# A mixer block and a hybrid layer on one core: row loads placed later in SP's program, and the last squares of a norm added on VectorE

## What is computed

```
# first block
m = sigmoid(ga) * (ya @ w_a_out) + sigmoid(gb) * (yb @ w_b_out)      # "wa", "wb"
x = x + m @ w_o                                                      # "wo"
gate = sigmoid(rmsnorm(x, ple_norm_g) @ w_ple_gate)                  # "gate"
x = x + gate * (p @ w_ple_proj)                                      # "proj"
# second block
mod = silu(c) @ w_ada + b_ada          # 2048 -> 3 * 2048, one row of c
shift, scale, gate = split(mod, 3)
h = rms_norm(x, g) * (1 + scale) + shift
... attention and retention from h @ w_in, then @ w_out
```

## Time and profile before

| what | value |
|---|---|
| time, median of 3 | 2500.03 us (2499.55 to 2504.28) |
| time of the profiled execution | 2501.74 us |
| its span, first to last instruction | 2500.2 us |
| granted TensorE clock, mean | 0.998 |
| PE busy | 2482.1 us (99%) |
| DVE busy | 1586.4 us (63%) |
| ACT busy | 975.8 us (39%) |
| POOL busy | 150.5 us (6%) |
| loads of modulation rows | 192 |

### The profile page before, as it was taken

How to read it: one execution, slowest core, us unless ns; L and a number is a source line. 1 busy time by engine, 2 the same in 40 slices (tenths; PEclk the granted TensorE clock), 3 DMA queues, 4 the chain that set the end, 5 groups by cost and what they waited for, 6 DMA issues and landing times.

```text
span 2500.2 us, 34300 instructions
## 1 busy us (share of the span) xinstructions
PE 2482.1 (99%) x13766; PEld 2112.9 (85%) x13766; DVE 1586.4 (63%) x2608; ACT 975.8 (39%) x1331; POOL 150.5 (6%) x195
## 2 busy tenths in 40 slices
PE   9999999999999999999989999999999999999999
PEld 8888888888889999988868788888888888888888
DVE  7656744567698888777677763585356555665435
ACT  6633325333344434432222353443344444444423
POOL 0011110012100000000001203200000000000001
PEclk9999999999999999999999999999999999999999
DMA  5333333333434434498688633336222344333532
GB/s 192 110 97 96 92 108 94 96 92 102 129 93 161 134 129 138 139 338 273 244 278 295 231 93 101 93 93 187 85 76 76 95 116 108 107 107 115 177 101 101
DMA packets 226686, 343.30 MB, mean 137 GB/s; under 512 B 68128, under 2 KB 87456, under 8 KB 223072
## 3 DMA queue, kind: packets, MB, share of 16 engines
q1 hardware_dynamic: 220480, 329.33, 42.0%
q10 hardware_dynamic: 1728, 8.81, 0.9%
q0 software_dynamic: 4320, 2.99, 0.5%
HBM read 308.01 MB, written 20.97 MB: 132 GB/s over the span
## 4 chain that ended last, share of the span: by engine, by line
PE 98%; DVE 1%; DMA 1%; issue 0%; ACT 0%; POOL 0%; SPq 0%; DVEq 0%; ACTq 0%; POOLq 0%
PE bank L397 79%; PE bank L558 4%; PE bank L557 4%; PE bank L556 4%; PE bank L1715 1%; PE bank L1714 1%; PE bank L1713 1%; PE bank L1039 0%; DMA RAW<-in_w_o 0%; PE bank L1098 0%; PE bank L1023 0%; DMA SG<-gates_dram 0%; POOL AC L2860 0%; PE bank L1101 0%; PE bank L1066 0%
## 5 line engine op out<-in xcount | busy, mean ns | idle before, releaser
L397 PE MATMUL bank<-XH,WL 128*128 128x512 f32 x2392 | 926.3, 389 | 8.5 <-DVE WL L470 8.5
L397 PE MATMUL bank<-XH,WH 128*128 128x512 f32 x2392 | 930.1, 391 | 0.0
L397 PE MATMUL bank<-XL,WH 128*128 128x512 f32 x2392 | 925.4, 389 | 0.0
L470 DVE TENSOR_TENSOR WL<-RAW,WH 128x1024 fp32r<-128x1024 f32 x366 | 454.5, 1243 | 487.2 <-ACT WH L432 486.6
L432 ACT CAST WH<-RAW 128x1024 fp32r<-128x1024 f32 x366 | 383.3, 1048 | 856.0 <-PE bank L397 765.3
L397 PEld LDWEIGHTS bank<-XH,WL 128*128 128x128 f32 x2392 | 449.5, 188 | 103.0 <-DVE WL L470 9.8
L397 PEld LDWEIGHTS bank<-XH,WH 128*128 128x128 f32 x2392 | 449.8, 188 | 92.6 <-issue 0.2
L397 PEld LDWEIGHTS bank<-XL,WH 128*128 128x128 f32 x2392 | 449.6, 188 | 92.3 <-issue 0.5
L397 PE MATMUL bank<-WH,XL 128*128 128x512 f32 x384 | 149.4, 389 | 0.0
L397 PE MATMUL bank<-WH,XH 128*128 128x512 f32 x384 | 149.4, 389 | 0.0
L397 PE MATMUL bank<-WL,XH 128*128 128x512 f32 x384 | 149.4, 389 | 0.0
(11 more groups left out here) (389 smaller groups left out, 3015.7 us busy)
## 6 DMA issues: line engine op xcount, KB each, us to landing
RAW<-in_w_in SPq DMA_DIRECT2D x239, 512.0 KB, 3.8
RAW<-in_w_in SPq DMA_DIRECT2D x130, 256.0 KB, 3.0
ASX<-in_w_ada SPq DMA_DIRECT2D x108, 256.0 KB, 5.5
AST<-in_w_ada SPq DMA_DIRECT2D x84, 256.0 KB, 5.4
RAW<-in_w_o SPq DMA_DIRECT2D x32, 512.0 KB, 5.9
RAW<-in_w_gate SPq DMA_DIRECT2D x32, 512.0 KB, 3.8
RAW<-in_w_out SPq DMA_DIRECT2D x32, 512.0 KB, 3.8
gates_dram<-OUT ACTq DMA_DIRECT2D x8, 1024.0 KB, 4.5
```

Of the source, the lines that this page charges most:

```text
L397: ins = nc.tensor.matmul(bank[b][:, cols], l, r[:, cols], start=first, stop=final)
L470: nc.vector.tensor_tensor(low_of(m), RAW[:, m % NRAW], high_of(m).bitcast(F32), ALU.subtract).then_inc(lo.sem, lo.step(m))
```

## The change

It has three parts.

1. `ada_sp` gets nine empty pieces after its first seven rows, so that each later row load stands that much later in SP's program. With it the first of the four loads of SG moves from the list of reloads (`reload_rest`) to the beginning of wb 0, as the other three stand.
2. POOL adds squares 1 to 12 only. Squares 13, 14 and 15 lie in GT buffers 1, 2 and 3; DVE adds the second and third to the first and the sum to AC (`last_squares_dve`), and PE waits for DVE there.
3. The four adds of `modulation_dve` stand behind the proj groups on DVE and no longer ahead of them.

```
@@ ada_sp
         load_c(1)
         yield
+        yield from idle(9)
         for n in range(NADA, 192):
             yield from load_ada(n)
@@ new
+    def last_squares_dve():
+        V.wait_ge(act, (yield act, ("sq1", 14)))
+        nc.vector.tensor_tensor(GT[:, 1], GT[:, 1], GT[:, 2], ALU.add).then_inc(dve.sem, dve.step(("sq1", 14)))
+        V.wait_ge(act, (yield act, ("sq1", 15)))
+        V.wait_ge(dve, (yield dve, ("sq1", 14)))
+        nc.vector.tensor_tensor(GT[:, 1], GT[:, 1], GT[:, 3], ALU.add).then_inc(dve.sem, dve.step(("sq1", 15)))
+        V.wait_ge(pool, (yield pool, ("acc1", 12)))
+        V.wait_ge(dve, (yield dve, ("sq1", 15)))
+        nc.vector.tensor_tensor(AC[:, 0], AC[:, 0], GT[:, 1], ALU.add).then_inc(dve.sem, dve.step("acc1"))
@@ pe
-                T.wait_ge(pool, (yield pool, ("acc1", 15)))
+                T.wait_ge(dve, (yield dve, "acc1"))
                 ones_sum(b, AC[:, 0], ("r_ple", "sum"))
@@ dve_program
         yield from turns.finish(turns.specials)
         turns.pace = 1.0
-        yield from modulation_dve()
+        yield from last_squares_dve()
         for g in range(4):
             yield from dve_dense(("proj", g))
             ...
+        yield from modulation_dve()
         V.wait_ge(dve, (yield dve, "mod"))
@@ pool_program
-        for j in range(1, 16):
+        for j in range(1, 13):
@@ sp
-            Y.wait_ge(dve, (yield dve, ("ada", ADA_ZONES[0] - 1)))
-            load_gate(ld["sgb"], 0, SG[:, :, :], 4)
-            yield
         def next_gate(g):
             yield
-            Y.wait_ge(ev_d, (yield ev_d, (("wb", g - 1), 3)))
+            if g:
+                Y.wait_ge(ev_d, (yield ev_d, (("wb", g - 1), 3)))
+            else:
+                Y.wait_ge(dve, (yield dve, ("ada", ADA_ZONES[0] - 1)))
             load_gate(ld["sgb"], g, SG[:, :, :], 4 + g)
             yield
```

More of the change, by code:

```diff
@@ L2981, in sp @@
         for g in range(4):
-            if g:
-                turns.chores.append(next_gate(g))
+            turns.chores.append(next_gate(g))
             if g == 1:
```

## The result

The changed kernel takes **2530.19 us** (median of 4 executions, 2526.64 to 2531.14) against 2500.28 us for the kernel before on the same chip: ratio 1.0114, 95% interval 1.0096 to 1.0131, so 24 to 33 us slower. I had forecast 2497 with a range of 2489.5 to 2505. The profiled execution took 2531.14 us.

The account below looks back on a forecast made before the run. PE was taken as the bound, busy 2482.1 of 2500.2 us. Terms -10.4 + 9.8 - 3.15 and +0.8 for the clock gave -3 us: 2498.7 for the profiled execution, 2497 against the median, range 2489.5 to 2505.

Parts of the forecast that it names:

- What the lag takes away: In wo 0, PE's waits for DVE's late WL shrink to 0.9 us, a gain of 10.4 us.
- The squares: Before the sum of ones, PE can sum 4.85 us after the first bank add, not 8.0: gain 3.15 us.
- The modulation at no cost: Behind proj, the four small adds cost nothing, since DVE waits for ACT there; without that cover, 2 us.
- what it adds: In wo 1 to 3, fourth rows come late; DVE ends 7.0 us behind, costing 9.8 us before the sum.
- PE doesn't feel it: In wo, a WL may be some 9.1 us late without stalling PE; DVE's lag was put at 8.1 at most.
- Nothing else in wa and wb changes: In wa and wb, PE waited for nothing and the lag was to cost nothing there.
- L: Time from a row load's issue to its landing in wo 1 to 3, taken as 4.5 us.
- A stretch of three gives back up to 2.5: In wo, DVE when behind runs three rows between WLs in 2.97 us against PE's 5.44, recovering up to 2.5.
- Each row is asked for in the stretch before: In wa and wb, with at most three rows between two WLs, each row is requested one stretch before use.
- The end of the rows: After wo 3, the last rows follow the last WL, so bank adds begin at E + 10.0: cost 9.8 us.
- PE stalls in wo: Rival: with landing at 5.0 to 5.5 us, PE stands at WLs in wo, 3 to 11 us slower; chance 0.26.
- my first rival: Rows come in time if landing is under 4.2 us: time falls 8 to 11 us, 2489 to 2492; chance 0.24.

Follow-up runs that it names:

- e12: The kernel before with a lag of 5 pieces and the gate's load among SP's chores, squares and modulation as before: 2490.92 us.
- e3: The changed kernel with a lag of 5 pieces in place of 9, rows asked for 7 pieces ahead of use: 2487.33 us.
- e1: The changed kernel with the lag alone undone; squares on DVE, modulation behind proj and the gate's load among the chores stay: 2497.92 us.
- e8: The changed kernel with a lag of 5 pieces and the modulation's four adds back in their old place: 2487.77 us.
- e10: The changed kernel with the lag of 9 pieces for rows up to 97 (wa and wb) only, then 5: 2498.30 us.
- e11: The changed kernel with a lag of 5 pieces up to row 97, then 9 from row 98 on (wo): 2515.59 us.
- e4: The changed kernel, lag still 9, with only the first half of each row loaded from the eighth on (with exceptions): 2509.20 us.
- e2: The kernel before with the lag of 9 pieces and the gate's load among the chores, squares and modulation as before: 2533.07 us.

## Why the prediction was wrong

The time was 30 us off, and the sum of its terms shows where.

- **What the lag takes away: right.** -10.4 us forecast, 0.9 us of waiting left; e12 has -11.6 and 0.8. SG "near 1224" holds for lags that keep the rows in time (1226.75 in e3); in the changed kernel itself it was issued at 1241.74, since SP waits for DVE's WLs and those were late.
- **The squares: right.** From the first bank add to the sum 4.85 us forecast, 5.0 in the changed kernel and 5.1 in e1, for 8.0 before. That is worth 2.9 us in e1, and with the 1.3 of clock that the prediction puts on this wait, which goes, 4.2; measured in e1 were 4.2 (1.8 to 6.3).
- **The modulation at no cost: right, and it was a small gain** (0.6 to 0.8 us by the profile of e8, too little for the times to show).
- Had the rows been in time, these terms and the clock give 2501.74 - 10.4 - 3.15 - 1.3 = 2486.9. The profiled execution of e3 took 2486.82.
- **The step that failed is "what it adds": that DVE's waits for rows stay within what PE's queue covers ("PE doesn't feel it"), with "Nothing else in wa and wb changes".** PE takes 376.6 us from wa to proj and not 348.9 (359.3 - 10.4): 27.7 us lost where the forecast had none. Of that 9.4 are in wa and wb (e10), 14.5 in wo (e11), and 3.8 come only where both have the lag. Three things in the step were wrong:
  1. **L was undersized.** I took 4.5 us, from two rows in a nearly empty queue, over the median of 5.5 at the same place. It was 5.4 over all rows of wo 1 to 3, and 5.3 in e3 too; the fourth rows, for which L stands in the sum, were started 5.3 us after their issue at the median. The median stood in the rows. e4, where the same rows came after 4.5, takes 21 us less than the changed kernel. But 4.5 is the forecast's own L, and e4 is still 7 us above before and not 3 below: the size of L isn't the whole error.
  2. **"A stretch of three gives back up to 2.5"** was wrong: DVE can run a stretch in 2.97 us only if the next rows are there, and they are asked for at the head of that stretch, 3 us ago. In wo 1 to 3 of the changed kernel the first rows of stretches of four wait 19.6 us in 9 places, beside the 30.1 us of the fourth rows; with half rows they still wait 14.9 us in 9. That fits e4's loss at an L at which I had a gain; no run takes these waits away alone.
  3. **"Each row is asked for in the stretch before"** was taken to mean in time. In wa and wb rows take 5.8 us at the median and up to 13.4, and the row behind the 1 MB gate shown above 7.95 (1162.96 to 1170.91), but a stretch is 5.44 us at PE's rate and 3 when DVE catches up from a group's banks. From 1060 to 1240 us DVE waits for rows 41.8 us in 20 places. Besides, "at most three rows between two WLs" was miscounted: at a pace of 1.6 a stretch has 3.2 rows on average, so in wb some have four, and the fourth row of the one at 1213.08 made DVE's longest wait, 6.17 us.
- **The end of the rows: nearly right.** Bank adds 10.0 us after the end of wo 3 forecast, 12.1 measured; PE's wait at the sum 9.4 forecast, 11.5 measured. The last WL ended 5.3 us after the start of proj for 3.9 forecast, 1.4 of the 2.1 us. This part of the walk held though DVE waited more than twice as long as forecast; I take it that this is since PE itself waits when a WL is late, so that DVE's lag behind PE can't grow much further. That isn't tested.
- DVE's waits for rows were to be 45 us and were 106.5.
- **The rival that came true** is the one that PE stalls in wo, with its price of 3 to 11 us for L of 5.0 to 5.5: right in kind, and its sign, waits of PE for WL in wo 2 and 3, is there. But it left out wa and wb and the first rows, and 30 us came of it.

The account of the profiled execution: 2498.7 forecast + 27.7 (from wa to proj) + 2.1 (bank adds) + 0.2 (the sum) + 1.7 (ahead of wa, not the change's) = 2530.4, for 2531.14 measured.

## What to carry to other kernels

A load that is issued in bursts, behind another engine's work, is early by bursts and not by pieces: count the time of the shortest burst interval that the user can reach when it catches up, and hold against it the landing time at that same place in the trace, its median and not its best rows. Slack that an engine is said to win back by hurrying is worth nothing if its data is asked for by that same hurry. And when a load's place is shifted, try the middle: here, with the squares on DVE throughout, everything from 5 to 9 pieces ahead was 15 us faster than the kernel before, 4 pieces 9 us, 12 pieces only the 4 us that the squares give, and 3 pieces was 30 us slower.

## What the runs showed of the hardware

- Halving the rows' bytes took 1.2 us off the median landing (5.4 to 4.2). The Trainium skill (page DMA: Bandwidth & Descriptors, section Anatomy of one DMA) gives 2.0 us fixed and then bytes over 436 GB/s, a fit for DMAs that GpSimd issues. The L = 3.3 of my first rival came from it. By that rate, as an estimate, 128 KB less saves 0.3 us in a row by itself. No run here tests it: these rows are issued by SP, three or four at a time and behind a unit of weights, while the core moved 223 to 240 GB/s (1300 to 1440 us). That each row also gained what the rows ahead of it in the burst gained would fit the 1.2 us, but isn't tested either.
- A wait of PE had two prices. After 3.13 us of waiting for WL (1211.2 to 1214.4) the granted clock was 0.56 for the next 3.5 us, near the lower of its two levels (1.2 of 2.4 GHz), and PE began 9 matmuls; after 2.37 us (before 1359.10) the clock was 1.00 and PE began 15:

```profile
1214.30:1217.80 3.50, 3.44 (x9) 2.78 (x10) 1.84 (x7) 0.00 (x0) 0.00 (x0) 0.56 0.51 154
...
1359.00:1362.50 3.50, 3.40 (x15) 2.83 (x16) 3.50 (x8) 0.00 (x0) 1.19 (x1) 1.00 0.62 178
```

  The length of the wait alone doesn't decide it: in e11 a wait of the same 2.37 us, before 1393.56, was followed by a clock of 0.54 and 9 matmuls in 3.5 us, and in e2 one of 2.36 us, before 1407.06, by matmuls of 0.63 us.

  Over the whole stretch up to proj three of PE's eleven waits for WL in the changed kernel (3.13, 2.69 and 2.38 us) were followed by five or six matmuls of 0.63 us. Counted over the 20 matmuls behind it (fewer where the next wait comes sooner), at 0.227 us each undisturbed, each of these three cost 1.7 to 1.9 us more than its length, 5.3 together; each of the other eight, and the one wait for WH, some 0.3 more. So the 18.9 us of waits beyond the 0.8 that is left in e3 (which cost 0.3 more too) come to 18.9 + 5.3 + 2.7 - 0.3 = 26.6 of the 27.7 us. 1.1 us stay unexplained.
